# Feed-forward products on TensorE: two token halves taken in turn at every pass, in place of one half after the other

## The reference, cut to what matters

```python
def causal_dwconv(u, prev, w, b):
    L = u.shape[1]
    full = jnp.concatenate([prev.astype(u.dtype), u], axis=1)
    out = b + sum(full[:, i:i + L] * w[i] for i in range(CONV_W))
    return out, full[:, -(CONV_W - 1):]

def conv_glu(h, prev, w_in, conv_w, conv_b, w_out):
    g, u = jnp.split(h @ w_in, [D_FF], axis=-1)
    gc, new_prev = causal_dwconv(g, prev, conv_w, conv_b)
    return (jax.nn.gelu(gc, approximate=False) * u) @ w_out, new_prev
...
    h = rmsnorm(x, norm_ffn[l])
    o, prev = conv_glu(h, ffn_prev0[l], w_ffn_in[l], ffn_conv_w[l], ffn_conv_b[l], w_ffn_out[l])
    x = x + o
```

## Time and profile before

| | before |
|---|---|
| median of three runs | 2545.51 us |
| lowest, highest | 2544.48, 2546.43 us |
| the profiled execution's own time | 2545.51 us |
| its span, first to last instruction | 2543.5 us |
| TensorE matmul busy | 2500.9 us, 98% of the span, 18342 passes |
| TensorE weight loads busy | 2424.4 us, 18342 loads |
| VectorE, ScalarE, GpSimd busy | 64%, 41%, 32% |
| passes of the seven-product units | 3 lines of 3248 each, 9744 of the 18342 |
| granted TensorE clock, mean | 0.999 |

### The profile page before, as it was taken

How to read it: one execution, slowest core, us unless ns; L and a number is a source line. 1 busy time by engine, 2 the same in 40 slices (tenths; PEclk the granted TensorE clock), 3 DMA queues, 4 the chain that set the end, 5 groups by cost and what they waited for, 6 DMA issues and landing times.

```text
span 2543.5 us, 44017 instructions
## 1 busy us (share of the span) xinstructions
PE 2500.9 (98%) x18342; PEld 2424.4 (95%) x18342; DVE 1636.4 (64%) x2666; ACT 1054.9 (41%) x1737; POOL 807.4 (32%) x532
## 2 busy tenths in 40 slices
PE   8999999999999999999999999999999999999999
PEld 6899999999999999999998998999999999999999
DVE  6735354588676666774625886666797676658754
ACT  6434342563333334232547766444543333333322
POOL 5222222253444443003522214323434444441002
PEclk9999999999999999999999999999999999999999
DMA  3111101032332326252213353212213333336522
GB/s 114 40 34 40 50 24 52 22 127 87 105 113 93 110 95 243 86 170 76 73 51 126 111 213 131 84 61 76 86 59 109 103 113 105 112 121 219 170 77 86
DMA packets 229681, 252.24 MB, mean 99 GB/s; under 512 B 16849, under 2 KB 178271, under 8 KB 228591
## 3 DMA queue, kind: packets, MB, share of 16 engines
q1 hardware_dynamic: 227087, 247.36, 29.4%
q10 hardware_dynamic: 2400, 2.10, 0.3%
HBM read 173.54 MB, written 75.89 MB: 98 GB/s over the span
## 4 chain that ended last, share of the span: by engine, by line
PE 82%; DVE 11%; issue 2%; ACT 2%; DMA 1%; POOL 0%; SPq 0%; DVEq 0%; ACTq 0%; POOLq 0%
PE ps L906 14%; PE ps L908 13%; PE ps L907 13%; PE ps L349 9%; PE ps L351 9%; PE ps L350 9%; PE ps L2853 3%; PE ps L2838 1%; PE ps L1714 1%; PE ps L1715 1%; PE ps L1716 1%; PE ps L1727 1%; PE ps L1809 1%; PE ps L1792 1%; PE ps L2821 1%
## 5 line engine op out<-in xcount | busy, mean ns | idle before, releaser
L1581 POOL TENSOR_TENSOR wlo<-wraw,whi 128x1024 fp32r<-128x1024 f32 x78 | 192.3, 2465 | 440.1 <-DVE s_raw L1268 440.1
L314 POOL TENSOR_TENSOR wlo<-wraw,whi 128x2048 fp32r<-128x2048 f32 (+1 forms) x21 | 94.3, 4489 | 555.6 <-ACT whi L307 526.2
L906 PE MATMUL ps<-hh,whi 128*128 128x264 f32 x928 | 264.7, 285 | 5.8 <-DVE wlo L1309 3.5
L907 PE MATMUL ps<-hl,whi 128*128 128x264 f32 x928 | 263.9, 284 | 0.0
L908 PE MATMUL ps<-hh,wlo 128*128 128x264 f32 x928 | 263.8, 284 | 0.0
L349 PE MATMUL ps<-hh,whi 128*128 128x352 f32 x648 | 218.8, 338 | 0.6 <-ACT cqr L3188 0.3
L593 DVE TENSOR_TENSOR xT<-xT,ps 128x352 f32<-128x352 f32 x288 | 147.7, 518 | 101.7 <-PE ps L351 101.5
L351 PE MATMUL ps<-hh,wlo 128*128 128x352 f32 x648 | 208.2, 321 | 0.0
L350 PE MATMUL ps<-hl,whi 128*128 128x352 f32 x648 | 207.9, 321 | 0.0
L906 PEld LDWEIGHTS ps<-hh,whi 128*128 128x128 f32 x928 | 174.7, 188 | 7.4 <-DVE wlo L1309 4.6
L1581 POOL TENSOR_TENSOR s_lo<-s_raw,s_hi 128x512 fp32r<-128x512 f32 x80 | 157.6, 1970 | 60.0 <-ACT s_hi L1102 60.0
(11 more groups left out here) (473 smaller groups left out, 8629.1 us busy)
## 6 DMA issues: line engine op xcount, KB each, us to landing
wraw<-w_ffn_in SPq DMA_DIRECT2D x88, 512.0 KB, 3.8
s_a<-hf SPq DMA_DIRECT2D x44, 528.0 KB, 3.2
wraw<-w_ffn_out SPq DMA_DIRECT2D x44, 512.0 KB, 3.9
s_t<-h SPq DMA_DIRECT2D x16, 1056.0 KB, 4.5
hflat<-s_t SPq DMA_DIRECT2D x16, 1056.0 KB, 6.1
h<-s_a SPq DMA_DIRECT2D x12, 1056.0 KB, 5.8
wraw<-w_gla_in SPq DMA_DIRECT2D x24, 512.0 KB, 4.4
s_x<-xT SPq DMA_DIRECT2D x6, 1408.0 KB, 5.5
```

Of the source, the lines that this page charges most:

```text
L314: pool.tensor_tensor(lo[:, 0:cols], raw[:, 0:cols], hi[:, 0:cols].bitcast(F32), ALU.subtract).then_inc(S("w_lo"), 1)
L906: nc.tensor.matmul(out, w_[0], x_[0], start=first, stop=False, skip_group_check=True)
L907: nc.tensor.matmul(out, w_[0], x_[1], start=False, stop=False, skip_group_check=True)
L1581: return pool.tensor_tensor(lo[:, cols], raw[:, cols], hi[:, cols].bitcast(F32), ALU.subtract)
```

## The change

The loop over the two halves s moves from the outside of `product` to the inside. Before, all twelve passes of half 0 ran into the first bank, then all twelve of half 1 into the second. After it, each of the three passes of a step k is done for half 0 and at once for half 1, so that the bank changes at every pass, and the same 128x128 weight is loaded for four passes running (high weight: high activation of both halves, low activation of both halves) and then, as low weight, for two. The number of matmuls and of weight loads, their shapes, operands and sums, the waits ahead of a product and the increment on its 24th pass are as they were. The order of the additions into one bank is the same as before.

```diff
         def product(bank, w, x, more=False):
 
-            for s in range(2):
-                for k in range(HK):
-                    w_ = [v[:, k, :] if len(v.shape) == 3 else v[:, k * P:(k + 1) * P] for v in w]
-                    x_ = [v(k, s) for v in x]
-                    out, first = ps[:, bank + s, 0:HH], k == 0 and not more
-                    nc.tensor.matmul(out, w_[0], x_[0], start=first, stop=False, skip_group_check=True)
-                    nc.tensor.matmul(out, w_[0], x_[1], start=False, stop=False, skip_group_check=True)
-                    last = nc.tensor.matmul(out, w_[1], x_[0], start=False, stop=(k == HK - 1), skip_group_check=True)
+            for k in range(HK):
+                w_ = [v[:, k, :] if len(v.shape) == 3 else v[:, k * P:(k + 1) * P] for v in w]
+                first = k == 0 and not more
+                for part, (a, b) in enumerate(((0, 0), (0, 1), (1, 0))):
+                    for s in range(2):
+                        last = nc.tensor.matmul(ps[:, bank + s, 0:HH], w_[a], x[b](k, s), start=(first and part == 0),
+                                                stop=(k == HK - 1 and part == 2), skip_group_check=True)
             return last
```

## The result

| | before | after |
|---|---|---|
| median | 2545.41 us (8 runs, 2544.48 to 2547.45) | 2552.47 us (8 runs, 2552.03 to 2553.08) |
| ratio, 95% interval | | 1.0028 [1.0019, 1.0037] |
| profiled execution, its span | 2545.51, 2543.5 us | 2552.47, 2550.6 us |
| one unit, first pass to first pass | 20.413 us | 20.560 us |
| mean step inside a product | 121.61 ns | 122.34 ns |

The change costs 7.1 us, 0.28%. The forecast was no change; the time lies inside the stated range (2537 to 2553), near its upper end, and on the side of the slower rival.

A forecast was written before the change was run, and what follows sets the result against it. The prediction took TensorE's own pace, the distance between two passes, as the bound. Work 0, waits 0, switch 0 and step 1.0 rounded to 0 gave no change, 2545.5 us, with a range of 2537 to 2553 us.

The forecast's parts named there:

- the slower rival: Step to the other half of the same tile is dear, as moving reads run on: +14.1 us, 2559.6 us; chance 0.09.
- What bounds the kernel: Seven-product units are bound by TensorE's own pace, 121.5 ns a pass; 9744 passes, 1184 us, come under the change.
- Work, waits and readers, cover of the weight load: Same matmuls and loads, signals as before, each load hidden beside the pass before with 12 ns in hand: 0 us each.
- The bank switch: 8932 passes get a new PSUM bank switch ahead of them: taken as 0, between -1.1 and +1.8 us, lower end -11.5.
- The faster rival: Same-bank accumulation in a steady stream costs something that a switch takes away: -11.5 us, 2534.0 us; chance 0.11.
- Same weight, other half: Steps keeping the weight while moving columns go on to the other half: +1.0 us, rounded to 0; other end +14.1 us.
- The clock: Granted clock stays up, as the change makes no holes; rival that it falls: +1089 us, 3635 us, chance 0.01.

The follow-up runs named there:

- e5: Kernel before with only the weights in the changed kernel's order; moving columns as before, bank changed once in the middle: 2545.36 us, 1.0001 of before.
- e1: Kernel before with its order of weights and activations kept, but the PSUM bank changed at every pass: 2545.23 us, 0.9999 of before.
- e7: Changed kernel with the halves going there and back, so the half changes at four of a step's six passes, not all six: 2544.66 us, 0.9998 of before.
- e2: Changed kernel's order of weights and activations, but the bank changed only once, in the middle of a product: 2552.52 us, 1.0028 of before.
- e6: Kernel before with only the moving columns in the changed kernel's order; weights as before, bank changed once: 2551.41 us, 1.0024 of before.
- e8: Changed kernel with halves still in strict turn, but both high-activation passes done ahead of the low-activation one: 2551.60 us, 1.0026 of before.
- e9: Changed kernel with half 1 read from column 256 of its tile in place of 264: 2553.94 us, 1.0033 of before.
- e13: Changed kernel with each pair of passes started with half 1, then half 0: 2548.08 us, 1.0012 of before.
- e14: Changed kernel with halves still in turn, but four of six passes going to the other half of the other tile: 2551.96 us, 1.0027 of before.
- e3: Kernel before with three passes of half 0, then three of half 1, at each step k: 2541.63 us, 0.9985 of before.
- e16: Kernel before with every pass reading the same 264 columns of the product's first tile: 2534.78 us, 0.9959 of before.

## Why the prediction was right or wrong

**What bounds the kernel: right.** The units are bound by TensorE's distance between two starts. The loss is there and nowhere else: 7.0 us by the units' own lengths, of 7.1.

**Work, waits and readers, cover of the weight load: right.** 18342 matmuls and loads, the same three waits at nearly the same sizes. One reading under the last was off: single steps go down to 115 ns in both kernels, so that 6 ns and not 12 were in hand over the 109 ns of the load; no hole came of it. e5 shows in addition that in the up projection a weight loaded for four passes running has the same pace as one that alternates.

**The bank switch: right.** 0 was taken, with bounds of -1.1 and +1.8 us and a far one of -11.5. e1 has the switch alone at 0.9999 [0.9990, 1.0008], with the very unit of before. The faster rival falls with it. The shorter step from product to product on which it was built (120.32 ns) is no matter of banks: e1 has 120.33, and after has the same change of bank there but 122.62.

**Same weight, other half: here the prediction failed.** The term had two ends, +1.0 and +14.1 us; the near end was taken, and +7.1 us came, which is half of the far end. That the time still fell into the stated range, by 0.5 us, is owed to the width that was given for the slower rival and not to the sum, which had nothing for this term. Two things were wrong in its working.

- The kinds of step were priced as if a step's length belonged to its two passes. They were named by the weight and the line ("same weight", line 906 to 907), and the weight turned out to have no part in it in the up projection, and a small one in the down projection (e5). What counts most are the moving reads, and by their whole sequence: one step is 123.75 ns in after and 121.45 in e7.
- Long steps were taken to be "made up by short ones around them", so that a unit keeps its length. They are not in full: in before a unit is 38 pieces of 6.67 ns above its floor, 0.25 us, and what looked like a fixed 121.5 ns a pass was 120.0 ns and a surplus that the order sets. The trace of before could hardly tell the two apart, since all its products have the same order.

**The slower rival: right in sign, not in its mechanism.** It said that the step to the other half is dear, for 4872 steps at 2.9 ns, "because the two moving reads run on into each other". The first half holds in this much: turns of the halves at every pass cost (after, e2, e6, e8, e9, e13, e14). The steps that it named, from half 0 to half 1 of one tile, are 122.18 ns on average in after, 0.6 ns over the mean of before and not 2.9; the other steps of after, which it left alone, are 122.51. The reason given falls: with a third of the reads that run on, e14 loses as much. Put on its 4872 steps, the loss is 7.1 us / 4872 = 1.46 ns a step, over the 1.05 ns from which the rival decides. Its unit of 20.65 us came as 20.56.

**The clock: right.** The granted clock stayed at 1.00, its upper level, in every window shown of after and of the experiments. By the rule of the Trainium skill, page "TensorE: Matmul & The Clock Gate", section "A second HAM failure mode: psum-queue depth-cycling", cycling through the banks would have let the clock go to and fro; here no hole opens between passes, and e1 with its bank change at every pass has the time of before.

**What the prediction said of itself held.** It named as its weakest point that the trace has no stretch of switching at every pass. For the bank that didn't matter; for the columns, which switch along with it, it was all that mattered. The chance of 0.10 for slower was too low for a term whose two ends lay 13 us apart and whose near end rested on steps of another kind.

## What to carry to other kernels

Where TensorE has no holes, loop order is not free though work and waits are the same: another order of the same passes moved this kernel by 10.8 us between e3 and after, and most of what the change cost was the order of the moving reads. Before a loop over PSUM banks goes inside, ask what else turns along with the bank; here the bank was free and the operand that came along was not. A mean step in a steady stream holds only for the order in which it was taken, so the pace of a new order is measured in a stretch of that order, or its far bound keeps a real chance.

## What the runs showed of the hardware

- In the steady units of the up projection a pass of 264 columns with its own weight load starts 120.0 ns after the one before when the moving reads stay in one place (e16), at the clock's upper level. With reads from many places it is 121.1 (e3, 20.347 us / 168) to 122.7 ns (e9, 20.620 us / 168).
- The surplus there comes in whole pieces of 6.67 ns a unit, from 28 (e3) to 69 (e9) in 168 passes, alike for all these units of a layer.
- The accumulating bank can change at every pass for nothing (e1: 0.9999). Loading the same weight for four passes running gains nothing over another order of loads (e5: 1.0001); in the down projection that order cost 0.05 us in a unit of 20.44 us.
- The Trainium skill, page "TensorE: Matmul & The Clock Gate", section "Back-to-back issue gap", gives N / 2.4 + 2.5 ns for the gap of an isolated matmul of N columns, and says that in a stream of weight loads and matmuls both set the spacing. For 264 columns the formula gives 112.5 ns, an estimate by that page; the stream here has 120.0 ns at the least (e16), and the measurement decides.
